# Nine sums over partitions: halves added on VectorE, one full-precision product on TensorE

## The reference

```python
def rmsnorm(x, g):
    xf = x.astype(jnp.float32)
    y = xf * lax.rsqrt(jnp.mean(xf * xf, axis=-1, keepdims=True) + EPS)
    return (y * g.astype(jnp.float32)).astype(x.dtype)

# at the start of each hybrid layer
p = split_columns(rmsnorm(x, norm_g) @ w_in)
# on each head of 256 channels of the matrix LSTM
y_ml = rmsnorm(hm, ml_norm_g.reshape(ML_HEADS, ML_HD)).reshape(b, s, ML_W) * jax.nn.silu(p['ml_z'])
```

## Time and profile before

| | us |
|---|---|
| median of 3 timed runs | 1157.02 (1156.82 to 1157.35) |
| profiled execution | 1150.74 |
| span of the profile | 1148.9 |
| TensorE busy, matmuls | 1133.3 (99%) |
| GpSimd busy | 837.5 (73%) |
| VectorE busy | 694.5 (60%) |
| ScalarE busy | 656.3 (57%) |
| mean granted clock of TensorE | 0.996 |

### The profile page before, as it was taken

The page is one execution under the profiler, slowest core; times in us unless marked ns, Lnnn a source line. Parts: engine busy times, 40 slices in busy tenths (PEclk is TensorE's granted clock), DMA queues, the critical chain, the costliest instruction groups (busy, mean ns, idle before and its releaser), DMA issues.

```text
span 1148.9 us, 22855 instructions
## 1 busy us (share of the span) xinstructions
PE 1133.3 (99%) x8978; PEld 1065.6 (93%) x8978; DVE 694.5 (60%) x1257; ACT 656.3 (57%) x1093; POOL 837.5 (73%) x1087
## 2 busy tenths in 40 slices
PE   8999999999999999999999999999999999999996
PEld 6788998999988799899999999999789999999996
DVE  5786644466577765254747655556858457655554
ACT  7666854575677577346647444446566446444443
POOL 6988798679598979976876665667756784756562
PEclk9999999999999999999999999999999999999998
DMA  8553344445454534544565656554534554565550
GB/s 308 191 171 133 111 175 163 169 163 205 161 166 169 171 119 142 184 152 164 183 211 191 221 182 217 187 198 149 183 117 150 199 194 166 187 215 189 186 182 37
DMA packets 64123, 199.89 MB, mean 174 GB/s; under 512 B 6608, under 2 KB 17936, under 8 KB 64016
## 3 DMA queue, kind: packets, MB, share of 16 engines
q1 hardware_dynamic: 62192, 195.31, 49.0%
q10 hardware_dynamic: 1824, 3.11, 0.8%
HBM read 196.57 MB, written 1.84 MB: 173 GB/s over the span
## 4 chain that ended last, share of the span: by engine, by line
PE 95%; DVE 2%; ACT 1%; POOL 1%; DMA 1%; issue 0%; ACTq 0%; DVEq 0%
PE ps L1620 50%; PE ps L1678 20%; PE ps L1668 13%; PE ps L1636 2%; PE ps L1830 2%; DVE ring L951 1%; PE ps L1924 1%; POOL ring L348 1%; PE ps L1904 1%; PE ps L1934 1%; DMA x<-in_x 1%; PE ps L1865 1%; PE ps L1925 0%; PE ps L2063 0%; PE ps L1804 0%; ACT xs L472 0%
## 5 line engine op out<-in xcount | busy, mean ns | idle before, releaser
L348 POOL TENSOR_TENSOR ring<-raw,ring 128x256 fp32r<-128x256 f32 x1032 | 809.5, 819 | 282.6 <-ACT ring L455 282.3
L1620 PE MATMUL ps<-xs,ring 128*128 128x256 f32 x5040 | 599.6, 278 | 0.4 <-POOL ring L348 0.3
L1620 PEld LDWEIGHTS ps<-xs,ring 128*128 128x128 f32 x5040 | 582.5, 188 | 9.1 <-issue 6.3
L455 ACT ACTIVATE ring<-raw 128x1024 fp32r<-128x1024 f32 x364 | 378.1, 1053 | 89.1 <-PE ps L1678 48.9
L951 DVE TENSOR_TENSOR ring<-raw,ring 128x1024 fp32r<-128x1024 f32 x106 | 157.4, 1485 | 129.2 <-ACT ring L455 128.8
L1678 PE MATMUL ps<-ys,ring 128*128 128x256 f32 x2016 | 235.5, 276 | 0.0
L1678 PEld LDWEIGHTS ps<-ys,ring 128*128 128x128 f32 x2016 | 231.7, 188 | 0.0
L1668 PE MATMUL ps<-ring,xs 128*128 128x512 f32 x672 | 167.3, 401 | 2.3 <-DVE ring L951 2.3
L1668 PEld LDWEIGHTS ps<-ring,xs 128*128 128x128 f32 x672 | 123.9, 190 | 32.0 <-issue 3.8
L785 ACT ACTIVATE ys<-ca 128x256 fp32r<-128x256 f32 x44 | 18.4, 419 | 106.5 <-DVE ca L1414 106.5
L1263 DVE SCALAR_TENSOR_TENSOR ca<-ps,par,ca 128x253 f32<-128x253 f32 (+2 forms) x96 | 45.9, 478 | 35.8 <-ACT ca L541 34.4
(11 more groups left out here) (270 smaller groups left out, 969.2 us busy)
## 6 DMA issues: line engine op xcount, KB each, us to landing
raw<-in_w SPq DMA_DIRECT2D x364, 512.0 KB, 3.4
y<-bias_rows SPq DMA_DIRECT2D x6, 256.0 KB, 4.4
out_y<-y SPq DMA_DIRECT2D x4, 256.0 KB, 2.5
const<-in_const SPq DMA_DIRECT2D x1, 896.0 KB, 10.2
x<-in_x SPq DMA_DIRECT2D x3, 256.0 KB, 7.3
bias_rows<-lg ACTq DMA_DIRECT2D x1, 768.0 KB, 6.2
dec<-in_wT ACTq DMA_DIRECT2D x1, 512.0 KB, 3.6
qke<-in_ln ACTq DMA_DIRECT2D x1, 512.0 KB, 4.5
```

The costliest lines, as they stand in the source:

```text
L348: last = pool.tensor_tensor(ring[:, g % RING, 1, part], raw[:, g % RAW, part], ring[:, g % RING, 0, part].bitcast(F32), ALU.subtract)
L455: act.activation(ring[:, g % RING, 0, :], raw[:, g % RAW, :], ACT.Copy).then_inc(S["hi"], 1)
L1620: last = mm(ps[bank][:, half * T:(half + 1) * T], ring[:, slot % RING, wp, (at + k) * P:(at + k + 1) * P], rhs(k, xp), start=(first and i ...
```

## The change

`add_squares` gets a fourth addition of 128x256 behind the third: it adds the second half of `sqs[:, 0:512]` to the first, and signals TensorE only then. `sum_squares` keeps one product of 256 columns. A new VectorE step, `ml_square_sum(g)`, waits for ScalarE's squares of group g, adds the second tile of each head to the first (128 x 2 x 256, in place in `mq`) and signals a new semaphore, `hsq_sum`. `ml_squares` waits for that one and keeps one product of 512 columns. VectorE's table gets `ml_square_sum(0)` at slot 63 ahead of `y_tile(3)`, and `ml_square_sum(1)` at slot 67. The last norm is not touched.

```diff
--- before.py
+++ after.py
@@ -261,7 +261,7 @@
         gl_ps gl_x gl_abs gl_ln gl_cum lev_d lev_e lev_q lev_k lev_ps lev_ev levx_ev
         gout gout_ev gsq gssq gvar grms idx_ps idx_relu idx_used pen
         dsq dvar drms k_scaled q_fac tokT dqk_in rows_hi rows_lo bias_r pick_in dl_ps dl dl_max dl_e dl_p dT dT_ev dpv dpv_ev
-        conv_out conv_e mqk_in ms mp mnum num_ev den den_sq hsq hssq hvar hrms
+        conv_out conv_e mqk_in ms mp mnum num_ev den den_sq hsq hsq_sum hssq hvar hrms
         sum_out x_new ffn_e ffn_h a_ps a_max a_e a_p a_T a_T_ev a_pv a_pv_ev
         at_done wT_in wT_cut ln_in ge_t ge_e ge_done ln_v ln_r vln sg sg_done mo_e merged stored""".split()
         S = {n: sem(n) for n in names}
@@ -965,11 +965,9 @@
 
                 for b in range(1, 4):
                     dve.wait_ge(S["sq"], n * 4 + b + 1)
-                    ins = tt(ps[3][:, :] if b < 3 else sqs[:, 0:512], ps[3][:, :], sqs[:, b * 512:(b + 1) * 512],
-                             ALU.add)
-                    if b < 3:
-                        step(ins)
-                ins.then_inc(S["sq_sum"], 1)
+                    step(tt(ps[3][:, :] if b < 3 else sqs[:, 0:512], ps[3][:, :], sqs[:, b * 512:(b + 1) * 512],
+                            ALU.add))
+                tt(sqs[:, 0:T], sqs[:, 0:T], sqs[:, T:2 * T], ALU.add).then_inc(S["sq_sum"], 1)
 
             def factor(n, copy=False):
 
@@ -1289,6 +1287,12 @@
                     step(stt(e, e, DEN_MAX, ps[5][:, 0:T], ALU.min, ALU.max))
                     stt(e, ps[5][:, 0:T], -1.0, e, ALU.mult, ALU.max).then_inc(S["den"], 1)
 
+                def ml_square_sum(g):
+
+                    dve.wait_ge(S["hsq"], it * 2 + g + 1)
+                    sq = mq[:, 4 * g:4 * g + 4, :].rearrange("p (h c) t -> p h c t", h=2)
+                    tt(sq[:, :, 0, :], sq[:, :, 0, :], sq[:, :, 1, :], ALU.add).then_inc(S["hsq_sum"], 1)
+
                 def ml_mean(g):
                     dve.wait_ge(S["hssq"], it * 2 + g + 1)
                     dve.wait_ge(S["den_sq"], it + 1)
@@ -1338,8 +1342,8 @@
                         47: [(ml_weight, 2)], 48: [(ml_denominator, 1), (gla_norm, 0)], 49: [(ml_weight, 3)],
                         50: [(gla_norm, 1)], 51: [(ml_denominator, 2)],
                         53: [(ml_denominator, 3)], 60: [(y_tile, 0)], 61: [(y_tile, 1)], 62: [(y_tile, 2)],
-                        63: [(y_tile, 3)], 64: [(ml_mean, 0)], 65: [(ml_norm, 0)],
-                        68: [(ml_mean, 1)], 69: [(ml_norm, 1)]}
+                        63: [(ml_square_sum, 0), (y_tile, 3)], 64: [(ml_mean, 0)], 65: [(ml_norm, 0)],
+                        67: [(ml_square_sum, 1)], 68: [(ml_mean, 1)], 69: [(ml_norm, 1)]}
                 for lv in range(LEVELS):
                     jobs.setdefault(18 + lv, []).insert(0, (level, lv))
                 jobs[18].insert(0, (top, 1))
@@ -1603,9 +1607,7 @@
             def sum_squares(n):
 
                 pe.wait_ge(S["sq_sum"], n + 1)
-                for c in range(2):
-                    last = mm(ps[4][:, 0:T], ones, sqs[:, c * T:(c + 1) * T], start=(c == 0), stop=(c == 1))
-                last.then_inc(S["ssq"], 1)
+                mm(ps[4][:, 0:T], ones, sqs[:, 0:T], start=True, stop=True).then_inc(S["ssq"], 1)
 
             PARTS = ((0, 0), (0, 1), (1, 0))
 
@@ -1926,14 +1928,12 @@
                     last.then_inc(S["mnum"], 1)
 
                 def ml_squares(g):
-                    pe.wait_ge(S["hsq"], it * 2 + g + 1)
+                    pe.wait_ge(S["hsq_sum"], it * 2 + g + 1)
                     if g:
                         pe.wait_ge(S["hvar"], it * 2 + 1)
                     sq = mq[:, 4 * g:4 * g + 4, :].rearrange("p (h c) t -> p h c t", h=2)
-                    for c in range(2):
-                        last = mm(ps[7][:, :].rearrange("p (h t) -> p h t", h=2), ones, sq[:, :, c, :],
-                                  start=(c == 0), stop=(c == 1))
-                    last.then_inc(S["hssq"], 1)
+                    mm(ps[7][:, :].rearrange("p (h t) -> p h t", h=2), ones, sq[:, :, 0, :],
+                       start=True, stop=True).then_inc(S["hssq"], 1)
 
 
                 jobs = {8: [(index_columns,), (index_logits, 0)],
```

## The result

The changed kernel takes 1168.37 us (median of 6 timed runs, 1162.34 to 1170.39) and the kernel before, on the same chip, 1156.88 us (6 runs, 1150.44 to 1157.35). The ratio is 1.0101, with a 95% interval of 1.0078 to 1.0125: 11.5 us slower. The forecast was 1161.8 us with a range of 1158.5 to 1167. The direction is right; the size is not, and the time lies above the range.

A forecast was written before the change was run, and what follows sets the result against it. TensorE, busy for 99% of the span, was taken to bound the kernel. Terms of -0.5 (norms), +6.0 (ml_squares), +3.3 (clock) and -4.0 (split) gave +4.8 us, 1155.5 profiled, 1161.8 with 6.3 carried over; range 1158.5 to 1167.

The forecast's parts named there:

- The place and the size of the wait: At slot 68 in each layer TensorE waits for VectorE's new sum: a stall of 4.7 us, +6.0 us net for both layers.
- The step that decides: Second ml_squares group, slot 68: VectorE's queue delays the sum to 253.45 us, while TensorE arrives at 248.88.
- Slot 64 hidden: First ml_squares group, slot 64: VectorE's sum ends by 236.5, before TensorE asks at 237.11; no wait, gain 0.86 us.
- The norms: Five sum_squares places: one product less gains 0.43 us each, stalls of 0.42 at norms two to four; about -0.5 us in sum.
- The clock behind the stalls: After each slot 68 stall TensorE's granted clock falls to 0.50, costing 1.65 us each: +3.3 us, ends none and twice that.
- The freed split: Mixer, after norm four: VectorE's split of 9.50 us finishes near 813, so TensorE's 2.35 us wait and slow clock go: -4.0 us.
- the rival of another cause: The split's 9.50 us are not from turns at the port and come back whole: +8.8 us, 1165.8; chance 0.12.
- this outcome among its rivals: Split at 811 starves again or anew (0.19), or its 9.50 us have another cause (0.12); 4.0 us not given back.
- carry-over of 6.3 us: The kernel before's timed median lay 6.3 us above its profiled run; the forecast added this to 1155.5, giving 1161.8.

The follow-up runs named there:

- wait_only: The kernel before, both products kept; TensorE's ml_squares waits for a mark VectorE sets at slots 63 and 67, nothing added: 1164.15 us, ratio 1.0095.
- squares_late: The changed kernel with the second ml_squares product at slot 70 instead of 68, and the second group's mean, root and norm moved behind it: 1159.18 us, ratio 1.0040.
- norm_sums_only: The kernel before with the fourth addition and one product at the five norms only, ml_squares as before: 1151.81 us, ratio 0.9996.
- add_from_psum: norm_sums_only with the norms' additions cut so that each has an operand in PSUM: 1150.48 us, ratio 0.9998 against the kernel before.
- wait_filled: The changed kernel with five overwritten products of constants on TensorE ahead of the wait at slot 68: 1158.90 us, ratio 1.0071 against the kernel before.
- late_four_passes: squares_late with each ml_squares product issued twice, four passes instead of two at slots 64 and 70: 1151.58 us, ratio 1.0007 against the kernel before.
- changed_again: The changed kernel, unaltered, run once more: 1163.04 us, ratio 1.0096 against the kernel before.
- four_passes: The changed kernel with each remaining product issued twice, new sums and waits kept: 1168.08 us, ratio 1.0133 against the kernel before.
- split_to_gpsimd: The kernel before with the VectorE split that took 9.50 us moved to GpSimd: 1155.81 us, ratio 1.0042.
- gpsimd_yields: The kernel before with GpSimd waiting, ahead of its pieces for one slot of the mixer, until VectorE has done its split: 1151.50 us, ratio 0.9974.
- the like pair: The profiles of the kernel before and of changed_again, both from the same group of run times; their spans differ by 10.6 us.

## Why the prediction was right and wrong

**The place and the size of the wait (right).** The step that decides was read from VectorE's queue, and `wait_only` and `squares_late` show it from both sides. It was 4.3 us each instead of 4.7: the sum began 0.15 us earlier and took 1.10 us, TensorE went on 0.05 us behind it instead of 0.15, and it arrived 0.16 us later than forecast. The 0.1 us expected there shows behind the first pass instead, and is in the clock's term.

**Slot 64 hidden (right).** No wait in either layer. But the step said "gain 0.86" and stopped there. The spacing behind it changed, for 96 matmuls at least: 0.4 us and, up to the next norm, 2.9 us in one layer.

**The norms (right).** In `norm_sums_only` the stalls at norms two to four are 0.28, 0.28 and 0.34 us up to the first pass and 0.1 us more behind it, together 0.39 to 0.45 against 0.42; the additions there took 0.74 to 0.80 us against the 0.76 assumed. (The working lets the addition get its turn at 315.25, although the piece that it reads runs until 315.33; that is 0.08 us.) `add_from_psum` shows the cause. The rule of the Trainium skill that the prediction drew on (SBUF — State Buffer, Who interferes with whom) holds for these additions, which took at most 0.87 us instead of 0.42 and so never lost more than one piece's time of 0.70.

**The clock behind the stalls (mechanism right, size off).** The term was 3.3 us, and both waits were followed by 1.2 GHz, but for 3.41 and 6.83 us: 4.2 us in one profile and 4.6 in the other, within the prediction's ends of nothing and 6.6. `wait_filled` shows that idle time brings it on. That the length was forecast from the one stretch that existed was the weak point. It does not even hold for waits like that one: `late_four_passes` waited 2.5 us in the mixer and did not fall at all.

**The freed split (wrong).** The step that failed is "the split then asks about 0.15 us earlier in a piece, where the operations of line 1414 get their turn at its end". Its first half came true: in the piece that was running, the split asked after 0.51 us, and before after 0.65. Its second half did not, there or at any other moment:

| kernel | asked after the train's start, us | split took | ended after the train's end |
|---|---|---|---|
| before | 19.52 | 9.50 | 1.09 |
| after | 19.56 | 9.62 | 1.07 |
| `changed_again` | 20.12 | 9.03 | 1.09 |
| `four_passes` | 20.55 | 8.62 | 1.09 |
| `split_to_gpsimd` | 25.39 | 11.96 | 1.08 |
| `gpsimd_yields` | 19.91 | 3.52 | 1.09 |

In the piece of 0.70 us that was running these are 0.65, 0.51, 0.45, 0.16, 0.25 and 0.38 us. The other eight profiles say the same: the split asked 19.5 to 20.0 us into the train and ended 1.08 or 1.09 us after its end. It was kept out until the train's end every time, at whatever phase it asked. What its end follows is the end of GpSimd's unbroken train, as `split_to_gpsimd` lengthened and `gpsimd_yields` shortened the train and the split followed both. That also answers the rival of another cause. The prediction had this outcome among its rivals, with 0.31 together, and took a single event's odd phase for its cause. The rule of the Trainium skill just named says that the loser waits until the other has finished; here it waited for the last of a dozen and more, so in this stretch the measurement goes beyond the rule. Why an operation of line 1414 gets its turn after one piece and this split not after twelve is open.

**The spacing (missing).** No term of the sum had it. It explains why the gain of 5.6 us in work did not show in `squares_late`, the one kernel that had all of it and no long wait: `late_four_passes` differs from it in the passes at four places and in the spacing alone. It probably explains the carry-over of 6.3 us from the profiled run to the median: with the first feed-forward network at wide spacing (some 1550 matmuls), the way from the third norm's passes to the fourth's takes 188.6 or 188.7 us, where it takes 181.9 before, so 6.7 to 6.8 us more. The profile of before was a narrow run and its median, by its time, a wide one. So the network's spacing is the likely difference between the two groups of run times. That each timed run of the slower group had the wide network isn't shown, since only profiled runs can be looked into. In the profiles of kernels whose times form two clear groups it fits; the times of `four_passes` and `wait_only` don't form any. On the second chip none of 21 runs of before was in the slower group. That carrying the 6.3 us over did little harm is luck: on the chip of the result most runs of both kernels were in the slower group, on the third chip neither median was.

From the forecast's +4.8 to the like pair's +10.6: +3.6 for the split, +1.3 for the clock, +1.8 for the spacing, -0.9 and -0.3 for shorter waits at slot 68 and at the norms, and 0.3 that no term has. On the chip of the result like runs lie nearly 12 us apart (1162.34 against 1150.44, and 1168.1 to 1170.4 against 1156.8 to 1157.4); what makes the last 1 us isn't shown.

What sets the spacing is open. Shown are the two values and what full-precision products of 512 columns do to them. At slot 64, which TensorE reaches at 113.3 and without a wait in both layers of all fourteen profiles, one product or three left 117.8 all ten times and two left 113.3 all eighteen times. At the second place the picture is less simple: two products without the slow clock left 113.3, two with it left 117.8 all three times, three turned 117.8 into 113.3, the six of `wait_filled` did so too, and one product left either value. At the norms, with 256 columns, single products did both.

## What to carry to other kernels

A low busy share says nothing about when an engine's queue reaches a new step: read from its timeline what stands in front of it, and put the step where the bound engine asks after that. An instruction taken from the bound engine is worth its length only if the instructions behind it keep their pace, so compare the distance between neighbours in both traces, not only waits. When run times come in two groups, find what tells the groups apart first, and compare like with like.

## What the runs showed of the hardware

- TensorE at a granted clock of 1.00 runs back-to-back matmuls of 256 columns at 113.3 or 117.8 ns from start to start, for hundreds on end, in the same program: 24 take 2.72 or 2.83 us from first to next. The Trainium skill (TensorE: Matmul & The Clock Gate, Wait — 56ns, not 53.3ns?) gives one spacing for back-to-back matmuls at 2.4 GHz, the columns over 2.4 GHz and about 2.5 ns. For 256 columns that makes 109 ns, an estimate from that page's figure; the traces are above it at both values. That section counts no weight load for each matmul, and here each has one (8960 of each after).
- A VectorE operation of 1.2 us with two SBUF inputs took 8.6 to 12.0 us beside GpSimd pieces of 0.70 us that followed each other without a gap, and was done 1.07 to 1.09 us after the last one in all fourteen profiles. Where GpSimd stopped for it after 32 pieces, it took 3.5 us.
- After waits of 2.3 to 2.5 us the granted clock fell to 0.50 in seven of nine profiles (not in `wait_only` and `late_four_passes`), after 1.8 us in the only case, after 3.0 us in one of two, after 4.1 to 5.8 us in all seven, and after 1.1 to 1.4 us in none of four. While it was at 0.50, matmuls of 256 columns came every 213 ns.
